# Chunked scan of a state-space layer: TensorE issues a head pair's outputs ahead of the row products of the pair two further on

## The chip, the cores and the metric

The kernel is one program on one core of a Trainium2 chip. The metric is device microseconds for one execution of the whole program. Three timed runs of the kernel before gave 2722.53, 2725.86 and 2726.41 us; their median, 2725.86 us, is the time that the change is measured against.

## The reference, cut to what matters

The program computes two transformer-like layers, for 512 tokens of width 1024: a stick-breaking attention layer with memory cross-attention and a convolutional feed-forward part, then a Mamba-2 layer and a sparse attention layer, each with a gated feed-forward part. Everything is fp32. The change touches the Mamba-2 scan only:

```
def ssd_scan(x, bm, cm, dt_raw, dt_bias, a_log):     # 32 heads of 64, 4 groups of 8 heads, state 128
    ...
        acs = jnp.cumsum(dtk * A, axis=1)
        seg = acs[:, :, None, :] - acs[:, None, :, :]
        decay = jnp.exp(jnp.where(causal, seg, -jnp.inf))            # one matrix per head
        xdt = xk * dtk[..., None]
        cb = jnp.einsum("blgn,bsgn->blsg", ck, bk)                   # one matrix per group
        y_intra = jnp.einsum("blsg,blsgj,bsgjp->blgjp", cb, decay, xdt)
    ...
    y = (y + d_skip[:, None] * xs)
    y = y * jax.nn.silu(z)
    y = rmsnorm(y in groups of 512 channels, norm_g)
    return y @ w_out
```

The kernel takes all 512 tokens as one chunk, so there is no state from an earlier chunk.

## The kernel before

Each engine has its own written-out instruction stream and they meet through semaphores; nothing is scheduled automatically. TensorE (PE) takes its instructions strictly in the order of the code, and so do ScalarE (ACT), VectorE (DVE) and GpSimd (POOL). An instruction that waits for a semaphore therefore holds up all that stands behind it on its engine.

The scan works through 16 pairs of heads. For a pair p the work goes from engine to engine:

- TensorE, `head_rows(hd)` (L1403, L1409), once for each of the two heads: the cumulative sums of the head are broadcast to all rows by seven matmuls, into one of two slots of three PSUM banks each. A slot must be free: ScalarE must have finished with the user two places back (`decay_exp`, or `cb_out` where that was a group matrix).
- ScalarE, `head_decay(hd)` (L1963): four exponentials from the slot into `decay`, a ring of four heads. From head 4 on it first waits for `pair_y`, that is until TensorE has finished the outputs of the pair two back, whose place in the ring it takes.
- VectorE, `mix(hd)` (L2605): `decay` times the group matrix `cbm`, in place (`mixed`).
- GpSimd: `skip` (L2926) and `xdt` (L2930) for the pair, in rings of two pairs, also behind `pair_y` of the pair two back.
- TensorE, `pair_output(pair)` (L1428, L1431): 32 small products into the one PSUM bank 6. It waits for `mixed`, `xdt_ready`, `skip_ready`, and for `y_gated` of the pair before, since that pair's result must have left bank 6.
- VectorE, `gate` (L2610): bank 6 times the gate, into `zt` (`y_gated`). ScalarE squares it (L1972), and TensorE adds the squares up in `sum_squares` (L1440), two pairs late.

Every fourth pair begins a group. `group_products` (L1393) makes the group matrix in a slot, and ScalarE copies it out (L1952); the next slot user but one waits for that copy. When four pairs are summed, ScalarE makes the group's inverse root (two activation table loads, L1979 and L1981), VectorE scales the four results with it (`full`, L2615), ScalarE writes a high part (L1986) and VectorE a low part (L2176, `low`). The output projection `ssm_out` (L694 to L696) follows the scan on TensorE and takes these parts.

TensorE's own order around the change is the loop in `scan` (L1451): in the turn of a pair it issues the row products of the pair two further on, then the outputs of the pair, then `sum_squares` for the pair two back.

Of the kernel before, what the change touches and what calls it, by code (L numbers as in the profile page):

```python
# [182 lines left out]
def build(nc, a, out):  # L183
# [505 lines left out]
    def _(pe):  # L689
# [8 lines left out]
        def banks_out(free=bank_free):  # L698

            pe.wait_ge(free, turns.seen.get(free.name, 0) + FREE0)  # L700
# [686 lines left out]
        def group_products(g):  # L1387

            n = ROW_USERS.index(("cb", g))
            row_slot_free(n)  # L1390
            for kb in (0, 1, 3, 2):
                bank, c0, _, w = decay_strip(n % 2, kb)
                last = nc.tensor.matmul(ps[:, bank, c0:c0 + w], bct[:, g, P * kb:P * kb + P],  # L1393
                                        bct[:, 4 + g, P * kb:SEQ], start=kb != 3, stop=True, skip_group_check=True)
            last.then_inc(cb_ready, 1)

        def head_rows(hd):

            n = ROW_USERS.index(("head", hd))
            row_slot_free(n)  # L1400
            for kb in (0, 1, 3, 2):
                bank, c0, _, w = decay_strip(n % 2, kb)
                nc.tensor.matmul(ps[:, bank, c0:c0 + w], pick[:, hd:hd + 1].to_broadcast([P, P]), acs_t[:, P * kb:SEQ],  # L1403
                                 start=kb != 3, stop=False, skip_group_check=True)
            for kb, twice in ((0, 1), (1, 2), (2, 1)):

                bank, c0, _, w = decay_strip(n % 2, kb)
                blocks = ps[:, bank, :].rearrange("p (b c) -> p b c", c=P)[:, 0:1 + 3 * (twice - 1):3, :]
                last = nc.tensor.matmul(blocks, causal_b[:], ident_b[:].unsqueeze(1).to_broadcast([P, twice, P]),  # L1409
                                        start=False, stop=True, skip_group_check=True)  # L1410
            last.then_inc(acs_rows, 1)

        def pair_output(pair):

            g, bank = pair // 4, 6
            pe.wait_ge(skip_ready, pair + 1)
            pe.wait_ge(xdt_ready, pair + 1)
            pe.wait_ge(mixed, 2 * pair + 2)
            if pair:
                pe.wait_ge(y_gated, pair)  # L1420
            for kb in range(TB):
                for part in range(2):
                    for side in range(2):
                        hd, half = 2 * pair + side, slice(HD * side, HD * side + HD)
                        x = tok[:, g, kb, HD * (hd % HPG):HD * (hd % HPG) + HD]
                        off, n = D_OFF[kb], SEQ - P * kb
                        if part == 0:
                            nc.tensor.matmul(ps[half, bank, P * kb:SEQ], xdt[:, pair % 2, kb, half], decay[:, hd % 4, off:off + n],  # L1428
                                             start=kb == 0, stop=False, skip_group_check=True)
                        else:  # L1430
                            last = nc.tensor.matmul(ps[half, bank, P * kb:P * kb + P], x, skip[:, pair % 2, side, :],  # L1431
                                                    start=False, stop=kb == TB - 1, skip_group_check=True)
            last.then_inc(pair_y, 1)

        def sum_squares(c):

            pe.wait_ge(y_squared, c + 1)
            if c % 4 == 0 and c:
                pe.wait_ge(squares_out, c // 4)
            nc.tensor.matmul(ps[:, 7, :], share[:], sq[:, c % 2, :], start=c % 4 == 0, stop=c % 4 == 3,  # L1440
                             skip_group_check=True).then_inc(squares_in, 1)

        def scan():

            pe.wait_ge(acs_lo, 1)
            pe.wait_ge(bc_copied, 8)
            banks_out()
            group_products(0)
            for hd in range(4):
                head_rows(hd)  # L1450
            for pair in range(HEAD_PAIRS):  # L1451
                ahead = pair + 2
                if ahead < HEAD_PAIRS:
                    if ("cb", ahead // 4 + 1) in SLOT_OF and ahead % 4 == 3:
                        group_products(ahead // 4 + 1)
                    head_rows(2 * ahead)
                    head_rows(2 * ahead + 1)
                pair_output(pair)
                if pair >= 2:
                    sum_squares(pair - 2)  # L1460
            sum_squares(HEAD_PAIRS - 2)
# [55 lines left out]
        feature_pairs(1, acth, actl, free=conv_done, out=False)  # L1517
        gates_and_sums()
        scan()
        ssm_out()  # L1520
        gated_ffn(scaled, mods=2)
# [1510 lines left out]
```

## Time and profile before

| quantity | value |
|---|---|
| median of three timed runs | 2725.86 us |
| the profiled execution's own time | 2727.47 us |
| its span in the profile | 2725.8 us |
| TensorE (matmuls) busy | 2560.2 us, 94% |
| VectorE busy | 1349.3 us, 50% |
| ScalarE busy | 1068.2 us, 39% |
| GpSimd busy | 206.5 us, 8% |
| scan, from its first group product to the first product of `ssm_out` | 1207.61 to 1349.75 us |

All times of the trace are microseconds from the span's start. A busy share of the whole program says little on one stage, so the scan is read by itself: its windows, its waits and its instructions in order of time. A pair's turn is measured from one `gate` (L2610) to the next, since that is what the end of the pair's outputs releases.

### The profile page before, as it was taken

Reading aid. Unit: us, or ns where it says so; the run is one execution under the profiler, and the core shown is the slowest. Engines: PE = TensorE matmul, PEld = TensorE weight load, DVE = VectorE, ACT = ScalarE, POOL = GpSimd, SP = SyncE. Lnnn points to the kernel's source line nnn. Section 1 sums busy time; section 2 is a strip of 40 time slices with the busy share of each in tenths; the row PEclk is TensorE's granted clock in tenths of the full one; section 3 lists DMA queues with packets and bytes.
Section 4 is the critical chain, followed back from the end, with each engine's and each line's share of the span. In section 5 each row is a group of like instructions: output and inputs, shape, how many; then the busy total and the mean of one; then the engine's idle time right before and its main releaser. Section 6 shows DMA issues by size and latency. Waiting matters only on the chain.

```text
span 2725.8 us, 35075 instructions
## 1 busy us (share of the span) xinstructions
PE 2560.2 (94%) x13316; PEld 2079.8 (76%) x13316; DVE 1349.3 (50%) x1870; ACT 1068.2 (39%) x1569; POOL 206.5 (8%) x249
## 2 busy tenths in 40 slices
PE   6979899999999989998899999999988889999999
PEld 5856588788887778774588888888875767888887
DVE  5764447678853365424535633244535454533323
ACT  2235532335552255435535333233424554533322
POOL 1101101010000000001101000010001111100000
PEclk8989999999999999999999999999979999999999
DMA  6740053435423222220024422322311000232232
GB/s 239 265 154 1 16 197 132 145 112 187 154 85 103 90 80 93 87 83 1 1 101 139 154 93 87 108 91 94 100 51 24 16 23 15 71 106 94 85 108 78
DMA packets 178691, 263.21 MB, mean 97 GB/s; under 512 B 8232, under 2 KB 127904, under 8 KB 178592
## 3 DMA queue, kind: packets, MB, share of 16 engines
q1 hardware_dynamic: 156608, 194.00, 21.6%
q0 software_dynamic: 15232, 58.72, 6.1%
q10 hardware_dynamic: 6752, 9.09, 1.0%
q8 instruction: 71, 1.16, 0.2%
q14 instruction: 28, 0.23, 0.0%
HBM read 255.51 MB, written 2.10 MB: 95 GB/s over the span
## 4 chain that ended last, share of the span: by engine, by line
PE 80%; DVE 8%; ACT 6%; issue 3%; POOL 2%; DMA 0%; ACTq 0%; DVEq 0%; SPq 0%; POOLq 0%
PE ps L694 22%; PE ps L696 21%; PE ps L695 21%; PE ps L1321 3%; PE ps L917 2%; ACT decay L1963 2%; DVE wlo L2172 1%; PE ps L971 1%; PE ps L1428 1%; PE ps L1237 1%; DVE actl L2176 1%; PE ps L1263 1%; DVE modulated L2255 1%; PE ps L889 1%; ACT whi L1552 1%
## 5 line engine op out<-in xcount | busy, mean ns | idle before, releaser
L2172 DVE TENSOR_TENSOR wlo<-raw,whi 128x2048 fp32r<-128x2048 f32 x180 | 412.2, 2291 | 713.9 <-ACT whi L1552 713.9
L694 PE MATMUL ps<-acth,wlo 128*128 128x512 f32 (+1 forms) x1888 | 702.7, 372 | 26.1 <-DVE actl L2176 12.5
L696 PE MATMUL ps<-acth,whi 128*128 128x512 f32 (+1 forms) x1888 | 695.8, 369 | 0.0
L695 PE MATMUL ps<-actl,whi 128*128 128x512 f32 (+1 forms) x1888 | 695.7, 368 | 0.0
L1552 ACT ACTIVATE whi<-raw 128x2048 fp32r<-128x2048 f32 x180 | 343.6, 1910 | 568.8 <-PE ps L696 568.8
L694 PEld LDWEIGHTS ps<-acth,wlo 128*128 128x128 f32 x1888 | 357.3, 189 | 89.6 <-DVE actl L2176 15.0
L696 PEld LDWEIGHTS ps<-acth,whi 128*128 128x128 f32 x1888 | 357.3, 189 | 59.7
L695 PEld LDWEIGHTS ps<-actl,whi 128*128 128x128 f32 x1888 | 357.5, 189 | 59.3 <-issue 1.2
L694 PE MATMUL ps<-whi,hid_l 128*128 128x512 f32 x528 | 207.7, 393 | 5.2 <-DVE conv_t L2431 3.4
L695 PE MATMUL ps<-wlo,hid_h 128*128 128x512 f32 x528 | 206.0, 390 | 0.0
L696 PE MATMUL ps<-whi,hid_h 128*128 128x512 f32 x528 | 206.0, 390 | 0.0
L2189 DVE SCALAR_TENSOR_TENSOR macc<-mraw,c_silu,macc 128x256 f32<-128x256 f32 x336 | 137.7, 478 | 0.0
L694 PE MATMUL ps<-whi,actl 128*128 128x512 f32 (+1 forms) x320 | 120.4, 376 | 3.3 <-DVE actl L2176 1.6
L694 PEld LDWEIGHTS ps<-whi,hid_l 128*128 128x128 f32 x528 | 99.6, 189 | 27.4 <-DVE conv_t L2431 3.9
L696 PE MATMUL ps<-whi,acth 128*128 128x512 f32 (+1 forms) x320 | 117.9, 369 | 0.0
L695 PE MATMUL ps<-wlo,acth 128*128 128x512 f32 (+1 forms) x320 | 117.8, 368 | 0.0
L695 PEld LDWEIGHTS ps<-wlo,hid_h 128*128 128x128 f32 x528 | 99.6, 189 | 20.9 <-issue 0.5
L696 PEld LDWEIGHTS ps<-whi,hid_h 128*128 128x128 f32 x528 | 99.4, 188 | 20.7
L1321 PE MATMUL ps<-diag,pn 128*128 128x128 f32 x640 | 92.4, 285 | 20.0 <-POOL diag L2997 14.8
L1321 PEld LDWEIGHTS ps<-diag,pn 128*128 128x128 f32 x640 | 80.0, 193 | 35.9 <-issue 28.3
L2176 DVE TENSOR_TENSOR pnt_l<-ps,pnt_h 128x512 fp32r<-128x512 f32 (+1 forms) x96 | 55.2, 600 | 89.0 <-ACT pnt_h L2074 89.0
L2431 DVE SCALAR_TENSOR_TENSOR conv_t<-ps,cols,conv_t 128x511 f32<-128x511 f32 (+1 forms) x88 | 63.5, 746 | 58.6 <-ACT conv_t L1792 55.1
(330 smaller groups left out, 3647.5 us busy)
## 6 DMA issues: line engine op xcount, KB each, us to landing
mraw<-in_mod_w POOLq DMA_DIRECT2D x48, 1024.0 KB, 5.5
raw<-in_ffn_w_in SPq DMA_DIRECT2D x44, 1024.0 KB, 4.9
raw<-in_ffn_up SPq DMA_DIRECT2D x22, 1024.0 KB, 4.9
raw<-in_ssm_w_in SPq DMA_DIRECT2D x20, 1024.0 KB, 5.0
raw<-in_ffn_w_out SPq DMA_DIRECT2D x20, 1024.0 KB, 4.8
raw<-in_sb_win SPq DMA_DIRECT2D x12, 1024.0 KB, 5.0
raw<-in_ffn_down SPq DMA_DIRECT2D x10, 1024.0 KB, 4.8
raw<-in_xa_wkv SPq DMA_DIRECT2D x8, 1024.0 KB, 5.0
```

Of the source, the lines that this page charges most:

```text
L694: nc.tensor.matmul(o, ll, rh, start=start, stop=False, skip_group_check=True)
L695: nc.tensor.matmul(o, lh, rl, start=False, stop=False, skip_group_check=True)
L696: return nc.tensor.matmul(o, lh, rh, start=False, stop=stop, skip_group_check=True)
L889: last = nc.tensor.matmul(ps[:, 6, 2 * u + j:2 * u + j + 1], macc[:, u, P * j:P * j + P], ones_c[:], start=True, stop=True, skip_group_che ...
L917: return nc.tensor.matmul(ps[:, bank, c0:c0 + keys_of(sb)], k_t[half, pair, P * sb:P * sb + P], q_t[half, pair, P * sb:SEQ], start=start, ...
L1321: last = nc.tensor.matmul(ps[:, 4 + (3 * n + r) % 2, P * b:P * b + P], pn[:, n % 2, off:off + P], diag[:, n % 2, tb, :], start=b == 0, sto ...
L1552: nc.scalar.activation(whi[:, slot, :], raw[:, slot, :], ACT.Copy).then_inc(hi_ready, 1)
L1963: last = nc.scalar.activation(decay[:, hd % 4, off:off + w], ps[:, bank, c0:c0 + w], ACT.Exp, bias=neg_acs[:, kb, hd:hd + 1])
L2172: nc.vector.tensor_tensor(wlo[:, slot, :], raw[:, slot, :], whi[:, slot, :].bitcast(F32), ALU.subtract) \
L2176: return nc.vector.tensor_tensor(dst, src, hi.bitcast(F32), ALU.subtract)
L2189: last = nc.vector.scalar_tensor_tensor(out=o, in0=w, scalar=c, in1=o, op0=ALU.mult, op1=ALU.add)
L2431: last = nc.vector.scalar_tensor_tensor(out=x, in0=ps[:, 2 * u + j, 0:SEQ - shift], scalar=w, in1=x, op0=ALU.mult, op1=ALU.add)
```

## The change

The call of `pair_output(pair)` goes from behind the row products (and the group product, in the turns that have one) to ahead of them. Nothing else is edited, no wait is added or taken away, and the instructions of ScalarE, VectorE, GpSimd and SyncE keep their order.

```diff
             for hd in range(4):
                 head_rows(hd)
             for pair in range(HEAD_PAIRS):
+                pair_output(pair)
                 ahead = pair + 2
                 if ahead < HEAD_PAIRS:
                     if ("cb", ahead // 4 + 1) in SLOT_OF and ahead % 4 == 3:
                         group_products(ahead // 4 + 1)
                     head_rows(2 * ahead)
                     head_rows(2 * ahead + 1)
-                pair_output(pair)
                 if pair >= 2:
                     sum_squares(pair - 2)
             sum_squares(HEAD_PAIRS - 2)
```

On TensorE, in the middle of the scan, the kernel before has this order from the end of one pair's outputs to the start of the next pair's (L1403 and L1409 are one head's row products, L1440 is the sum of squares, L1428 and L1431 are a pair's outputs):

```order
L1431 MATMUL ps<-skip,tok 64x128 x2
L1440 MATMUL ps<-sq,share 128x512 [waits y_squared]
L1403 MATMUL ps<-acs_t,pick 128x512 [waits decay_exp]
...
L1409 MATMUL ps<-ident_b,causal_b 128x128
L1403 MATMUL ps<-acs_t,pick 128x512 [waits decay_exp]
...
L1428 MATMUL ps<-decay,xdt 64x512 [waits mixed,y_gated,xdt_ready,skip_ready]
```

The changed kernel has this one at the same place of TensorE's stream:

```order
L1431 MATMUL ps<-skip,tok 64x128 x2
L1403 MATMUL ps<-acs_t,pick 128x512 [waits decay_exp]
...
L1409 MATMUL ps<-ident_b,causal_b 128x128
L1403 MATMUL ps<-acs_t,pick 128x512 [waits decay_exp]
...
L1440 MATMUL ps<-sq,share 128x512 [waits y_squared]
L1428 MATMUL ps<-decay,xdt 64x512 [waits mixed,y_gated,xdt_ready,skip_ready]
```

The sum of squares has gone from ahead of the row products to behind them, and what looks the same is not: the row products between the outputs of pairs p and p+1 are those of pair p+3 before, and those of pair p+2 now.

At the start of the loop on TensorE, behind the row products of heads 0 to 3, the outputs of pair 0 now stand ahead of the row products of head 4:

```order
 L1409 MATMUL ps<-ident_b,causal_b 128x128
+L1428 MATMUL ps<-decay,xdt 64x512 x2
+L1431 MATMUL ps<-skip,tok 64x128 x2
+L1428 MATMUL ps<-decay,xdt 64x384 x2
+L1431 MATMUL ps<-skip,tok 64x128 x2
+L1428 MATMUL ps<-decay,xdt 64x256 x2
+L1431 MATMUL ps<-skip,tok 64x128 x2
+L1428 MATMUL ps<-decay,xdt 64x128 x2
+L1431 MATMUL ps<-skip,tok 64x128 x2
 L1403 MATMUL ps<-acs_t,pick 128x512
```

All eight rows of a pair's outputs have moved up by the row products of two heads.

## Rows read from the trace of the kernel before

**Rows 1.** Window: length, busy PE, PEld, DVE, ACT, POOL, granted clock, DMA.
```profile
1226.40:1345.10 118.70, 95.85 (x686) 57.02 (x688) 68.28 (x60) 76.01 (x157) 24.25 (x28) 0.99 0.00 1
```

**Rows 2.** Waits from 1226.4 to 1350: waiter, releaser, total, times, longest.
```profile
ACT decay L1963 <- PE ps L1431: 47.8, 12, 6.3
PEld ps L1403 <- ACT decay L1963: 25.3, 20, 2.2
```

**Rows 3.** Timeline of one ordinary turn: start, duration, engine, line, count.
```profile
1241.21 1.08 PE L1428 MATMUL ps<-decay,xdt 128*64 128x512 f32 x4
...
1244.39 1.13 PE L1440 MATMUL ps<-sq,share 128*128 128x512 f32 x2
1244.51 0.69 DVE L2610 TENSOR_TENSOR zt<-ps,zt 128x512 f32<-128x512 f32 x1 [2.89 <-PE ps L1431]
...
1244.57 3.46 ACT L1963 ACTIVATE decay<-ps,neg_acs 128x512 f32<-128x512 f32 x8 [3.96 <-PE ps L1431]
...
1246.41 0.91 PE L1403 MATMUL ps<-acs_t,pick 128*128 128x512 f32 x4 [0.89 <-ACT decay L1963]
1246.46 3.10 DVE L2605 TENSOR_TENSOR decay<-decay,cbm 128x1280 f32<-128x1280 f32 x2 [1.26 <-ACT decay L1963]
...
1248.08 0.91 PE L1403 MATMUL ps<-acs_t,pick 128*128 128x512 f32 x4 [0.53 <-ACT decay L1963]
...
1249.15 1.08 PE L1428 MATMUL ps<-decay,xdt 128*64 128x512 f32 x4
```

**Rows 4.** Timeline of one turn with a group product.
```profile
1260.38 0.69 DVE L2610 TENSOR_TENSOR zt<-ps,zt 128x512 f32<-128x512 f32 x1 [2.89 <-PE ps L1431]
...
1262.28 2.43 PE L1393 MATMUL ps<-bct 128*128 128x512 f32 x8 [0.89 <-ACT decay L1963]
...
1266.15 0.91 PE L1403 MATMUL ps<-acs_t,pick 128*128 128x512 f32 x4 [0.58 <-ACT cbm L1952]
...
1270.52 0.69 DVE L2610 TENSOR_TENSOR zt<-ps,zt 128x512 f32<-128x512 f32 x1 [5.09 <-PE ps L1431]
```

**Rows 5.** Timeline of the start, to the first pair's gate.
```profile
1214.68 3.10 DVE L2605 TENSOR_TENSOR decay<-decay,cbm 128x1280 f32<-128x1280 f32 x2 [3.10 <-ACT decay L1963]
...
1218.49 1.54 PE L1403 MATMUL ps<-acs_t,pick 128*128 128x512 f32 x4
...
1220.25 1.52 PE L1403 MATMUL ps<-acs_t,pick 128*128 128x512 f32 x4
...
1226.44 0.69 DVE L2610 TENSOR_TENSOR zt<-ps,zt 128x512 f32<-128x512 f32 x1 [4.74 <-PE ps L1431]
```

**Rows 6.** Window at the start, columns as in group 1.
```profile
1224.00:1224.50 0.50, 0.50 (x8) 0.41 (x6) 0.00 (x0) 0.00 (x0) 0.00 (x0) 0.82 0.00 0
```

**Rows 7.** Timeline of the end of the scan and the first product behind it.
```profile
1336.26 0.69 DVE L2610 TENSOR_TENSOR zt<-ps,zt 128x512 f32<-128x512 f32 x1 [2.31 <-PE ps L1431]
...
1342.43 1.10 PE L1440 MATMUL ps<-sq,share 128*128 128x512 f32 x2 [1.99 <-ACT group_rstd L1979]
1343.46 0.20 PEld L1428 LDWEIGHTS ps<-decay,xdt 128*64 128x64 f32 x4 [0.76 <-issue]
...
1348.45 0.69 DVE L2610 TENSOR_TENSOR zt<-ps,zt 128x512 f32<-128x512 f32 x1 [3.43 <-PE ps L1431]
...
1349.75 0.79 PE L694 MATMUL ps<-whi,yl 128*128 128x512 f32 x1
```

**Rows 8.** Timeline: VectorE and ScalarE work that the later turns add.
```profile
1274.58 1.28 ACT L1979 ACT_TABLE_LOAD   x1
...
1278.51 3.46 ACT L1963 ACTIVATE decay<-ps,neg_acs 128x512 f32<-128x512 f32 x8
...
1286.99 2.26 DVE L2615 SCALAR_TENSOR_TENSOR zt<-zt,cols,group_rstd 128x512 f32<-128x512 f32 x2
```

**Rows 9.** Timeline behind the last pair, where VectorE has no GpSimd work beside it.
```profile
1349.06 2.06 DVE L2615 SCALAR_TENSOR_TENSOR zt<-zt,cols,group_rstd 128x512 f32<-128x512 f32 x3
...
1351.04 2.49 DVE L2176 TENSOR_TENSOR yl<-zt,yh 128x512 fp32r<-128x512 f32 x4
```

## The prediction, written before the changed kernel was run

> **What bounds the kernel now.** I read the waits of the scan first, then one ordinary turn and one group turn in order of time, then both ends, and the windows last, for the clock. The page's 94% of TensorE says nothing here: in the scan TensorE's matmuls are busy 95.85 of 118.70 us and ScalarE 76.01 [rows 1], so no engine is full. The waits name a ring: ScalarE's exponentials wait 47.8 us in 12 waits for the end of a pair's outputs, and the weight loads of the row products wait 25.3 us for the exponentials [rows 2].
>
> One turn shows how the ring closes [rows 3]. The outputs of a pair start at 1241.21 and release ScalarE at 1244.57, 3.36 us later. TensorE's next row products want a slot that these exponentials must first read: the first head's start at 1246.41, the second's at 1248.08, so 3.51 us after ScalarE began. The outputs of the next pair stand behind them in TensorE's order and start 1.07 us later, at 1249.15. The turn is 3.36 + 3.51 + 1.07 = 7.94 us. The reader is to see that these outputs needed nothing from those exponentials: their own two heads had been mixed a turn earlier. They are late only because of what stands in front of them. A turn with a group product takes 10.14 us, 1260.38 to 1270.52 [rows 4].
>
> **What the change does to an ordinary turn.** Nothing is added or removed; the terms are gaps. Behind the outputs of pair p now come the row products of pair p+2, not p+3. Their slots were read by the exponentials of pair p+1, a turn ago, so TensorE doesn't wait. The turn becomes TensorE's own work:
> - outputs, start to the next instruction's start, 1241.21 to 1244.39: 3.18 us [rows 3];
> - row products of two heads. The 1.07 us from a head's start to the outputs' start [rows 3] is the upper end for one. The lower end is 0.88: at half clock one head follows another after 1.76 us [rows 5]. I take 1.0 each, nearer to the row at full clock: 2.0 us;
> - sum of squares: 1.03 us, 1342.43 to 1343.46 [rows 7]. (Where it stands behind outputs it looks shorter, as its start overlaps their end.)
>
> Sum 6.2 us, against 7.94.
>
> The price of the move is on ScalarE: its exponentials for pair p+2 now wait for the outputs of p and also for the row products behind them, some 1.2 us. Does that come back? The chain from the end of outputs p is: row products 1.2, exponentials 3.5 (the second head's last, rows 3), mix of the second head 1.5 (half of 3.10), so pair p+2 is ready 6.2 to 6.3 us after outputs p end. It is needed at two turns less one set of outputs, 12.4 - 3.2 = 9.2 us. Slack 2.9 us. The other condition is bank 6: the gate stands on VectorE behind both mixes of the pair p+1, which end about at the end of outputs p (6.3 - 6.2), and takes 0.69; the next outputs start 3.0 us after that end. Slack some 2.2 us. Sums of squares wait for squares that are a turn old. GpSimd's work for a pair has a whole turn.
>
> **The group turns.** Outputs end, the group product starts at once; from its start to the second head's row products is 1262.28 to 1266.15 = 3.87 us, ScalarE's copy being on that path [rows 4]. Then 1.07 (head to next), 1.03 (squares) and 3.18 (outputs): 9.15 us against 10.14. In the first group turn there are no squares yet: 8.1. The gain is small here because the copy out of the slot stays in the path.
>
> **The sum.** From the first gate to that of pair 13 the trace has 13 turns, 1226.44 to 1336.26 = 109.8 us, which is 3 x 10.14 and 10 x 7.94 [rows 5, 7]. After: the first turn without squares 5.2, the group turns 8.1 + 9.15 + 9.15, nine ordinary turns 9 x 6.2 = 55.8. Together 87.4 us, 22.4 less.
>
> The end: before, pairs 14 and 15 take 1336.26 to 1348.45, 12.2 us, with a wait of 1.99 us for the group root [rows 7]. After: 6.2, and for pair 15 outputs 3.2, squares 1.0 and what is left of that wait. ScalarE comes to the root's first half 1.2 (row products) + 3.3 + 0.5 + 2.0 (table load and logarithm, half of the 3.93 from 1274.58 to 1278.51, rows 8) = 7.0 us after outputs 13, TensorE after 6.2: a wait of 0.8. Sum 11.2, a gain of 1.0.
>
> The start: outputs of pair 0 can go at 1218.4, where the row products of head 4 started at 1218.49; the mixes they need ended at 1217.8 [rows 5]. The granted clock is at half, the 1.2 GHz level, and comes back to 2.4 GHz at about 1224.2 (0.82 in that half microsecond, rows 6); TensorE is as busy until then as before, so I leave that moment where it is. So of 3.3 us of work at full clock 2.9 are done by 1224.2 and the gate comes at about 1224.6, not 1226.44: 1.8 us.
>
> 22.4 + 1.0 + 1.8 = 25.2 us. Each turn has hand-overs between kinds of instructions that no row shows in the new order; at 0.1 us in each of twelve they take back 1.2. I forecast 24 us. What follows the scan is TensorE's from 1349.75 on [rows 7], and its first two weight blocks lie in SBUF long before, so it shifts as a whole. The profiled execution's own time is 2727.47 us around a span of 2725.8; it would become 2703.5. On the median, 1.6 us lower, that is 2725.9 - 24 = 2701.9 us.
>
> **What could be dearer.** VectorE in turns from 7 on has mixes 2.9, gate 0.6, one `full` 0.7 and one `low` 0.6 (a third and a quarter of rows 9), 4.8 us. But two `full` beside GpSimd's work take 2.26 us [rows 8], and three without it 2.06 [rows 9]: the one that meets GpSimd costs 1.6, so 0.9 more. That is 5.7 of 6.2 us.
>
> The Trainium skill ("SBUF — State Buffer", section "Who interferes with whom") says that a VectorE instruction with two SBUF inputs contends with a GpSimd one that reads SBUF, and that whoever came first has the shared port for its whole instruction. The 1.6 us agrees. By that rule a shorter turn could make a mix lose such a stretch as well, 4.8 + 2 x 0.9 = 6.6 us, over TensorE's 6.2: 0.4 in each of nine turns, 4 us lost, 2706. It is counted within the second rival.
>
> **The rivals.**
> 1. TensorE fills its turns, -24 us: 2702. Its own range is 2699 to 2706: the row products at 0.88 or 1.07 each move 26 of them by 3 and 2 us, and the last pair's outputs may again take 5.0 us to their gate (1343.46 to 1348.45, rows 7) and not 3.3, which my sum has left out.
> 2. VectorE and ScalarE take over as the bound from turn 7 on. For it: turn 7, 11 and 15 have the root's 3.9 us on ScalarE [rows 8], which uses up most of the gate's 2.2 us of slack, and the mixes come nearer to GpSimd's work in a shorter turn. Against: the sums above, 5.7 us on VectorE. Priced by VectorE's fullest turn, mixes 2.9, gate 0.7, two `full` 2.26, `low` 0.6 and 0.7 of waiting, 7.1 us: nine turns at 0.9 more are 8 us, so -16: 2710.
> 3. The scan ends earlier and nothing behind it does, because the projection waits for something timed from elsewhere: 2726. Against it: DMA share is 0.00 through the scan [rows 1], so nothing is on the way that could be late.
> 4. Slower: the granted clock. In the scan it is 0.99 of full although TensorE pauses about 2 us in each turn, but at the start it is at half [rows 6]. At half clock a turn's 6.2 us are 12.4. It decides once more than 59 us of the scan are at half clock, for each such us costs half of one, and 24 + 5.5 us must be lost for a slower kernel. A whole scan so, some 100 us of work done in 200, would end at 2800. Against: the change takes pauses away.
>
> **How the numbers follow.** Chances: 0.75, 0.18, 0.05, 0.02. A difference under 0.2%, 5.5 us, can't be told from none here. The first two cases are faster by far more, and of the third's spread a little is too: faster 0.94, same 0.04, slower 0.02. The range takes the first case's and goes to the second's price and a little over: 2698 to 2711.
>
> **What would show it.** In the profile after, ScalarE's exponentials wait for L1409, not L1431; the 25.3 us of waits of L1403 for exponentials are gone but for the copies (L1952) in three turns; gates come 6.2 us apart, 9.2 in group turns; the scan's PE share goes from 0.81 to over 0.95. Rival 2 shows as TensorE waiting for L2605 or L2610 ahead of L1428 from turn 8 on. Gates under 6.0 or over 6.5 us apart in the early turns would mean that I mis-sized TensorE's own turn, and a wait for `mixed` in turns 2 to 6 that the chain of 6.3 us is wrong.

## The result and the profile after

Four runs of the changed kernel gave 2695.52 to 2700.37 us, median 2698.56, beside 2724.2 us for the kernel before in the same comparison: 25.6 us less, ratio 0.9903, 95% interval 0.9889 to 0.9917. A second build of it on another occasion gave 2697.47 against 2725.46 us, ratio 0.9902 (0.9886 to 0.9919). The forecast was 24 us less, 2701.9 us, in a range from 2698 to 2711. The first median is inside it, 0.6 us above its lower end; that of the second build is 0.5 us below it. Of the 3.3 us between 2701.9 and 2698.56, 1.7 are the kernel before, whose median was 2725.86 us when the forecast was made and 2724.2 us in the comparison; 1.6 are the change.

| | before | after |
|---|---|---|
| profiled execution, own time | 2727.47 | 2698.84 |
| span | 2725.8 | 2697.1 |
| first group product of the scan | 1207.61 | 1206.06 |
| first product of the projection | 1349.75 | 1320.18 |
| scan, between them | 142.1 | 114.1 |
| from there to the end of the span | 1376.1 | 1376.9 |

The spans differ by 28.7 us: 28.0 in the scan, 1.6 ahead of it and -0.9 behind it, which the change doesn't touch. Outside the scan, where no kernel of this document differs, the spans of all thirteen traces lie between 2577.0 us (squares first) and 2586.8 us (between heads). So the traces tell what happens in the scan more finely than the timed runs of the whole program do.

In the window of the scan (columns as in [rows 1]) TensorE is now busy for 108.23 of 113.73 us, 0.95, against 0.82 in the whole scan of the kernel before (0.81 without its start, [rows 1]). ScalarE went from 0.62 to 0.77, VectorE from 0.55 to 0.67:

```profile
1206.06:1319.79 113.73, 108.23 (x797) 69.14 (x798) 75.81 (x67) 87.41 (x178) 28.37 (x28) 0.97 0.03 11
```

The waits after, from 1200 to 1330 (columns as in [rows 2]):

```profile
ACT decay L1963 <- PE ps L1409: 14.2, 10, 3.7
...
DVE zt L2610 <- PE ps L1431: 3.8, 4, 1.7
...
PEld ps L1403 <- ACT cbm L1952: 3.3, 4, 0.9
PEld ps L1403 <- ACT decay L1963: 2.5, 3, 2.2
...
PE ps L1440 <- ACT group_rstd L1979: 1.1, 1, 1.1
```

ScalarE no longer waits for outputs, 47.8 us before, but for the row products behind them, 14.2 us. TensorE's loads for row products waited 28.0 us for the exponentials, 25.3 of them behind the first gate [rows 2]; 2.5 are left, 2.2 of them in one wait at the start. What still stops TensorE are the group copies and one wait for the group root.

One ordinary turn in the timeline after answers to [rows 3]:

```profile
1243.44 1.08 PE L1428 MATMUL ps<-decay,xdt 128*64 128x512 f32 x4
...
1246.62 0.89 PE L1403 MATMUL ps<-acs_t,pick 128*128 128x512 f32 x4
1246.74 0.69 DVE L2610 TENSOR_TENSOR zt<-ps,zt 128x512 f32<-128x512 f32 x1
...
1247.56 0.88 PE L1403 MATMUL ps<-acs_t,pick 128*128 128x512 f32 x4
1247.79 3.46 ACT L1963 ACTIVATE decay<-ps,neg_acs 128x512 f32<-128x512 f32 x8 [2.10 <-PE ps L1409]
1248.51 1.08 PE L1440 MATMUL ps<-sq,share 128*128 128x512 f32 x2
1249.52 1.08 PE L1428 MATMUL ps<-decay,xdt 128*64 128x512 f32 x4
```

TensorE has no wait in it. Outputs take 3.18 us to the next start, the first head's rows 0.94, the second's 0.95, the squares 1.01: 6.08 us, against 7.94. ScalarE starts its exponentials 4.35 us after the outputs' start, 3.36 before: that is the price of the move, and nobody is late for it.

In the later turns VectorE is nearly full, and a gate (the multiplication that takes a pair's outputs out of bank 6) no longer marks the end of the outputs, since it comes late. The timeline there:

```profile
1266.10 3.10 DVE L2605 TENSOR_TENSOR decay<-decay,cbm 128x1280 f32<-128x1280 f32 x2 [0.99 <-ACT decay L1963]
...
1267.97 1.70 POOL L2926 TENSOR_TENSOR skip<-ident,heads 128x256 f32<-128x256 f32 x1 [4.45 <-PE ps L1431]
...
1269.11 0.69 DVE L2610 TENSOR_TENSOR zt<-ps,zt 128x512 f32<-128x512 f32 x1
...
1270.72 1.08 PE L1428 MATMUL ps<-decay,xdt 128*64 128x512 f32 x4
```

The outputs ended at about 1267.9, the gate began at 1269.11, 1.2 us late behind two mixes, and ended at 1269.80, 0.9 us before the outputs of the next pair. So VectorE was close to being the bound and did not become it. I therefore read turns from one pair's outputs to the next, by their starts on TensorE. From the timelines, one kernel to a row (the edits follow below), in us; "first" is from the first group product to the outputs of pair 0, "last" from the last pair's outputs to the projection:

```
                      first  0-1   1-2   2-3   3-4   4-5   5-6   6-7   7-8   8-9   9-10  10-11 11-12 12-13 13-14 14-15 last   scan
before                14.54 11.13  7.93  7.94  7.94 10.14  7.93  7.93  7.93 10.21  7.93  7.94  7.93  7.93  4.23  6.27  6.29  142.1
after                 10.67  6.42  8.12  6.08  6.09  6.08  9.04  6.07  6.09  6.08  9.04  6.07  6.09  6.09  6.08  5.41  4.60  114.1
squares last          14.54 11.18  7.92 10.48 10.39 10.13 10.36 10.96 10.59 11.22  8.84 11.93 10.67 10.63  4.23  6.50  6.01  166.6
squares last, busy    14.55 11.14  7.93 10.47  8.85 10.28  8.84 11.94  9.24 10.28  8.84 11.00  8.85  8.84  5.53  4.97  5.90  157.5
squares first         10.69  6.43  8.12  6.03  6.04  6.04  8.98  7.69  6.04  6.02  8.98  7.71  6.03  6.02  6.03  7.17  5.39  119.4
between heads         12.81 10.34  6.26  6.26  6.25  8.40  6.25  7.81  6.25  8.41  6.26  7.79  6.25  6.25  5.16  5.34  4.60  120.7
first pair only       10.68 12.40  8.50  8.99  7.94 10.14  7.93  7.93  7.92 10.22  7.92  7.94  7.94  7.93  4.23  6.27  4.60  139.5
all but first         14.00  4.13  8.13  6.09  6.08  6.08  9.04  6.08  6.09  6.07  9.04  6.08  6.08  6.09  6.09  5.40  4.60  115.2
before, more rows     14.88 10.14  9.22  7.94  7.93 10.14  7.94  7.92  7.93 10.22  7.93  7.93  7.93  7.93  4.23  6.54  5.97  142.7
after, more rows      10.31  5.63  8.12  6.56  6.55  6.54  9.04  6.55  6.55  6.54  9.04  6.55  6.55  6.54  6.55  5.41  4.59  117.6
squares fill          10.67  6.46  8.12  6.08  6.09  6.08  8.18  6.10  6.36  6.08  8.19  6.09  6.37  6.08  6.09  4.13  5.65  112.8
fill and start        11.53  5.99  8.13  6.08  6.09  6.08  8.19  6.09  6.35  6.08  8.19  6.09  6.35  6.08  6.08  4.13  5.65  113.2
```

The gain of 28.0 us from the first two lines: 3.9 at the start and 23.4 in the 13 turns to pair 13 (110.8 to 87.4); 1.0 is lost in the two turns to pair 15 (10.5 to 11.5), because the outputs of pair 14 followed those of pair 13 at once before and have the last row products ahead of them now; and 1.7 is gained in the last stretch.

### The profile page after: what moved, and what is told of

Same layout as the page of the kernel before. It is cut to its first block, busy times and chain, and to the rows that moved or that the text cites. A ratio compares the mean times of both kernels' runs of the same rounds, so it can differ in the third digit from the quotient of the medians.

```text
span 2697.1 us, 35075 instructions
## 1 busy us (share of the span) xinstructions
PE 2552.4 (95%) x13316; PEld 2079.4 (77%) x13316; DVE 1347.8 (50%) x1870; ACT 1067.6 (40%) x1569; POOL 210.5 (8%) x249
## 4 chain that ended last, share of the span: by engine, by line
PE 81%; DVE 8%; ACT 4%; issue 3%; POOL 2%; DMA 0%; ACTq 0%; DVEq 0%; SPq 0%; POOLq 0%
PE ps L694 22%; PE ps L696 22%; PE ps L695 22%; PE ps L1321 3%; PE ps L917 2%; PE ps L1428 1%; DVE wlo L2172 1%; PE ps L971 1%; PE ps L1237 1%; PE ps L1403 1%; DVE actl L2176 1%; PE ps L1263 1%; DVE modulated L2255 1%; PE ps L889 1%; ACT whi L1552 1%
```

## The experiments

My theory: the kernel before is held by a ring that closes only through TensorE's order, the outputs standing behind row products that wait for the exponentials which the last outputs released. Moved ahead, they leave TensorE bound by its own work. Rivals: the sums of squares, which moved too; the start alone; VectorE or ScalarE as the new bound.

**Squares last.** The order before, with only the sums of squares moved.

```diff
+                if grouped:
+                    if pair >= 3:
+                        sum_squares(pair - 3)
+                    group_products(ahead // 4 + 1)
                 if ahead < HEAD_PAIRS:
-                    if ("cb", ahead // 4 + 1) in SLOT_OF and ahead % 4 == 3:
-                        group_products(ahead // 4 + 1)
                     head_rows(2 * ahead)
                     head_rows(2 * ahead + 1)
+                if pair >= 3 and not grouped:
+                    sum_squares(pair - 3)
                 pair_output(pair)
-                if pair >= 2:
-                    sum_squares(pair - 2)
+            sum_squares(HEAD_PAIRS - 3)
             sum_squares(HEAD_PAIRS - 2)
```

> The kernel before, with only the other thing that the change did to TensorE's order: each sum of squares goes behind the row products (in the three turns with a group product it goes ahead of them), while the outputs stay last in the turn. Theory (the ring through TensorE's order): a sum of squares that stood beside the wait for the exponentials now stands in the ring, so an ordinary turn grows from 7.94 by 0.92 us to 8.9 us, in some nine turns, and in two of them TensorE also waits for the group root, 1 us more: the kernel is 8 to 11 us slower than before, ratio 1.003 to 1.004. Rival (moving the sums of squares was part of the gain): faster than before by some us, turns under 7.9 us.

Measured: 2747.68 us against 2725.01, ratio 1.0083 (1.0064 to 1.0103), 22.7 us slower: the sign of the theory and twice its size. The squares' move earns nothing by itself. (What it is worth behind outputs that come first is the experiment after the next.) But ordinary turns are 10.4 to 10.7 us, not 8.9, except one of 8.84 us. The timeline of TensorE in one of them, and the windows over it (the eighth number, behind POOL's, is the granted clock):

```profile
1245.05 0.89 PE L1403 MATMUL ps<-acs_t,pick 128*128 128x512 f32 x4 [1.94 <-ACT decay L1967]
...
1246.72 1.50 PE L1403 MATMUL ps<-acs_t,pick 128*128 128x512 f32 x4 [0.54 <-ACT decay L1967]
...
1248.46 1.95 PE L1440 MATMUL ps<-sq,share 128*128 128x512 f32 x2
```

```profile
1245.00:1246.00 1.00, 0.95 (x7) 0.82 (x7) 0.90 (x1) 1.00 (x3) 0.00 (x0) 1.00 0.00 0
1246.00:1247.00 1.00, 0.46 (x4) 0.28 (x2) 0.89 (x2) 0.67 (x3) 0.00 (x0) 0.90 0.02 8
1247.00:1248.00 1.00, 1.00 (x4) 0.83 (x3) 1.00 (x1) 0.00 (x0) 0.00 (x0) 0.50 0.00 0
...
1250.00:1251.00 1.00, 1.00 (x5) 0.34 (x6) 0.00 (x0) 0.49 (x1) 0.00 (x0) 0.89 0.00 0
```

The clock falls to its 1.2 GHz level for some 3.4 us of the turn, while the second head's rows and the squares run, both in the ring. With the squares behind the rows TensorE pauses 1.94 us ahead of the first head's rows. In the kernel before the squares stood in that pause and left 0.89 us of it [rows 3], and the clock stayed; only its first turns have the long pause, for want of squares.

The turn of 8.84 us has the same pause, and there the clock stayed at full speed:

```profile
1313.00:1323.00 10.00, 7.52 (x57) 4.81 (x59) 5.55 (x5) 3.45 (x9) 2.15 (x2) 1.00 0.01 2
```

```profile
1319.18 0.90 PE L1403 MATMUL ps<-acs_t,pick 128*128 128x512 f32 x4 [1.94 <-ACT decay L1967]
...
1321.82 1.08 PE L1440 MATMUL ps<-sq,share 128*128 128x512 f32 x2
```

So the ring is as long as its terms say when the clock holds, and the clock does not fall behind each such pause.

**Squares last, busy.** The test of that: the same kernel, with products in the pause. They add to columns of the bank in which the sums of squares stand, so this kernel's output isn't the reference's.

```diff
+        def keep_busy():
+            for _ in range(3):
+                nc.tensor.matmul(ps[:, 7, 0:256], ident[:], causal6[:, 0:256], start=False, stop=True,
+                                 skip_group_check=True)
...
                 pair_output(pair)
+                if pair % 4 != 2:
+                    keep_busy()
```

> The kernel with the squares last (the outputs as before, sums of squares behind the row products) took turns of 10.4 us where the ring gave 8.9, and its granted clock was 0.83 in most windows. Here TensorE gets more work: three products of 256 columns, 1.3 us, directly behind each pair's outputs, into the sums' bank (so the sums of squares and the output aren't the reference's), in all turns but those in which ScalarE reads that bank. They fall in the 2 us in which TensorE waits for the exponentials. Theory (the miss was the clock, which falls because TensorE pauses in that wait and the work that follows is in the ring): the clock stays at 1.00, ordinary turns are 8.8 to 9.0 us, the kernel is 8 to 13 us slower than before, ratio 1.003 to 1.005, in spite of more work than the one without. Rival (the ring has another part that I missed): turns of 10.4 us and more, ratio 1.008 or above.

Measured: 2743.73 us against 2725.16, ratio 1.0061 (1.0044 to 1.0079), above the expected ratios. Its scan is 9.1 us shorter than without the extra work; of the whole program the timed runs show 4 us, with intervals that overlap, so the gain from more work is shown in the scan only. By turns the theory holds: behind pairs that got the work, the turns that have neither a group product nor a root are 8.84 or 8.85 us, one 9.24. Behind pairs 2, 6 and 10, which didn't, they are 10.47, 11.94 and 11.00 (the last two with the root's wait). I had forgotten those three turns in the expectation. In one turn with the work:

```profile
1254.64 1.56 PE L1438 MATMUL ps<-causal,ident 128*128 128x256 f32 x6
1256.66 0.91 PE L1403 MATMUL ps<-acs_t,pick 128*128 128x512 f32 x4 [0.45 <-ACT decay L1975]
...
1258.33 0.90 PE L1403 MATMUL ps<-acs_t,pick 128*128 128x512 f32 x4 [0.53 <-ACT decay L1975]
...
1259.30 1.08 PE L1446 MATMUL ps<-sq,share 128*128 128x512 f32 x2
1260.31 1.08 PE L1428 MATMUL ps<-decay,xdt 128*64 128x512 f32 x4
```

and the granted clock in the two windows around it, first over a turn without the work and then with it:

```profile
1243.00:1253.00 10.00, 7.51 (x48) 4.45 (x46) 3.67 (x3) 4.09 (x9) 1.62 (x2) 0.83 0.00 1
1253.00:1263.00 10.00, 9.02 (x72) 5.78 (x70) 3.68 (x3) 4.09 (x9) 1.62 (x2) 1.00 0.01 2
```

The second head's rows take 0.90 and the squares 1.08, not 1.50 and 1.95. So the ring is 7.94 + 0.91 = 8.85 us, as its terms say, and what was over was the clock. In this trace the clock fell in none of the turns that got the work (in the one of 9.24 us it was still down from the turn before).

**Squares first.** The changed kernel, with `sum_squares(pair - 2)` directly behind `pair_output(pair)`:

```diff
                 pair_output(pair)
+                if pair >= 2:
+                    sum_squares(pair - 2)
...
-                if pair >= 2:
-                    sum_squares(pair - 2)
```

> The changed kernel with each sum of squares moved back directly behind the outputs, ahead of the row products. Theory: TensorE is full in both orders, so ordinary turns stay at 6.1 us; but the sums for pairs 4 and 8 wait for ScalarE's group root, now with the row products behind them and not only outputs, 1 to 1.5 us in each of two turns. 22 us faster than before, ratio 0.992, 2 to 4 us behind the changed kernel. Rival (the place of the squares matters in each turn): a turn over 6.5 us, less than 18 us faster.

Measured: 2700.98 us against 2725.01, ratio 0.9916 (0.9894 to 0.9939); 24.0 us. Ordinary turns 6.03 us, and 7.69 and 7.71 in the two turns with the root, as the wait of 1.63 us shows:

```profile
1261.32 1.10 PE L1440 MATMUL ps<-sq,share 128*128 128x512 f32 x2 [1.63 <-ACT group_rstd L1979]
```

The scan is 5.3 us longer than in the changed kernel, a little more than I wrote, 3.2 in those two turns and most of the rest at the end (7.17 + 5.39 against 5.41 + 4.60). Where the squares stand is worth nothing in an ordinary turn, once the outputs are first. But these 5.3 us of the scan are what their place behind the row products earns in the changed kernel, by shorter waits for the group root and full clock at the end; the change's gain is not the outputs' move alone.

**Between heads.** The order before, with the outputs moved past one head's rows only:

```diff
                     head_rows(2 * ahead)
+                pair_output(pair)
+                if ahead < HEAD_PAIRS:
                     head_rows(2 * ahead + 1)
-                pair_output(pair)
```

> The kernel before, with the outputs moved up past one head's row products only: first head, outputs, second head, squares. Theory: the ring still closes through TensorE's order but over one head's exponentials: 3.36 + 1.84 + 1.07 = 6.3 us in an ordinary turn, 8.3 in a group turn (the copy of the group matrix no longer stands ahead of the outputs), about 7.7 in the two turns behind a group root. 20 to 23 us faster than before, ratio 0.992. Rival (the outputs must be ahead of all row products for TensorE to get past the wait): half the gain or less, turns of 7 us and more. Rival (TensorE's own work is the bound in both): the same turns as the changed kernel, 6.1 and 9.0 us.

Measured: 2704.97 us against 2725.01, ratio 0.9921 (0.9904 to 0.9937); 20.0 us. Turns 6.25, with a group product 8.40, with a root 7.80; 6.3, 8.3 and 7.7 were expected. One turn in the timeline of TensorE:

```profile
1242.09 1.08 PE L1428 MATMUL ps<-decay,xdt 128*64 128x512 f32 x4
...
1245.27 0.90 PE L1403 MATMUL ps<-acs_t,pick 128*128 128x512 f32 x4
...
1246.24 1.08 PE L1440 MATMUL ps<-sq,share 128*128 128x512 f32 x2
1247.28 0.90 PE L1403 MATMUL ps<-acs_t,pick 128*128 128x512 f32 x4
...
1248.34 1.08 PE L1428 MATMUL ps<-decay,xdt 128*64 128x512 f32 x4
```

The first head's rows start 5.19 us after the outputs did, which is 3.36 us to the exponentials and 1.83 for those of one head; their weight load waits 0.79 us for ScalarE. The outputs follow 1.06 us later. This experiment tells the ring's formula from "TensorE is full in any order", if by little: the turn is 0.17 us longer than TensorE's own 6.08 in the changed kernel and 0.22 us longer than the 6.03 of squares first. It is shorter in group turns, where the copy is out of the path.

**First pair only.** The order before, and for pair 0 the changed one.

```diff
+                if pair == 0:
+                    pair_output(pair)
...
-                pair_output(pair)
+                if pair > 0:
+                    pair_output(pair)
```

> The kernel before, with only the outputs of pair 0 moved ahead of the row products of head 4; all later turns as before. Theory: what the first gate gains (1.8 to 3.6 us) the second turn gives back, since the exponentials of pair 2 then wait for row products that stand behind the outputs: the second gate comes some 11 us after the first, not 10.1, and the kernel is 1 to 2 us faster than before, which the timing can't tell. Rival (the start is a gain of its own): 3 to 4 us faster, and the second gate 10.1 us behind the first.

Measured: 2725.52 us against 2725.01, ratio 1.000 (0.999 to 1.0009). In the trace pair 0 is 3.9 us early and the next three turns are 1.3, 0.6 and 1.1 us longer (in the last two the clock fell behind the long pause of the turns without squares); to the outputs of the last pair the whole is 1.0 us ahead of before. The start is not a gain of its own. (The scan of this trace is 2.6 us shorter than before, 1.7 of them in the last stretch, where the clock held; the timed runs show nothing of it.)

**All but first.** The complement: pair 0 as before, all others as changed (the two conditions above exchanged).

> The changed kernel with the outputs of pair 0 left behind the row products of heads 4 and 5, where they were before; all later turns as changed. Theory: nearly the whole gain is in the turns: 23 to 26 us faster than before, ratio 0.991, with ordinary turns of 6.1 us and the first gate as late as before. Rival (the start and the early return of the clock carry a seventh of the gain): 4 us and more behind the changed kernel.

Measured: 2699.64 us against 2725.84, ratio 0.9911 (0.9891 to 0.993); 26.2 us. The scan is 1.1 us longer than the changed kernel's: pair 0 comes 3.3 us later and the next turn is 2.3 us shorter, since pair 1 was ready long before.

**More rows, in both orders.** The widest row product of each pair's first head three times, same values, in the kernel before and in the changed one.

```diff
             for kb in (0, 1, 3, 2):
                 bank, c0, _, w = decay_strip(n % 2, kb)
-                nc.tensor.matmul(ps[:, bank, c0:c0 + w], pick[:, hd:hd + 1].to_broadcast([P, P]), acs_t[:, P * kb:SEQ],
-                                 start=kb != 3, stop=False, skip_group_check=True)
+                for _ in range(3 if kb == 0 and hd % 2 == 0 else 1):
+                    nc.tensor.matmul(ps[:, bank, c0:c0 + w], pick[:, hd:hd + 1].to_broadcast([P, P]),
+                                     acs_t[:, P * kb:SEQ], start=kb != 3, stop=False, skip_group_check=True)
```

> The kernel before with more work for TensorE: the first, 512 columns wide row product of each pair's first head is issued three times and not once (the repeats overwrite the same values). Theory: they fall in TensorE's wait for the second head's exponentials, 0.53 us in each turn, so 0.45 us of work costs nothing: turns stay at 7.94 us, the kernel within 2 us of before. Rival (TensorE's work already counts in the kernel before): turns of 8.4 us, 6 us slower.

> The changed kernel with the same repeats: the first row product of each pair's first head three times. Theory (TensorE is now full): each turn grows by the whole 0.45 us, from 6.1 to 6.55 us, 6 us in 14 turns; 18 to 21 us faster than before, ratio 0.993. Rival (VectorE or ScalarE bound the later turns): turns from 7 on stay at their length, 3 us or less in all.

Measured: before with them 2724.73 us against 2725.84, ratio 0.9997 (0.9987 to 1.0007), ordinary turns 7.92 to 7.94 (9.22 once, in an early one, where the clock fell). The repeats have filled the second wait, and the second head's rows start 1.68 us behind the first's, 1.67 before [rows 3]:

```profile
1251.65 1.36 PE L1404 MATMUL ps<-acs_t,pick 128*128 128x512 f32 x6 [0.89 <-ACT decay L1964]
...
1253.33 0.90 PE L1404 MATMUL ps<-acs_t,pick 128*128 128x512 f32 x4
```

After with them 2701.0 us, ratio 0.9916 (0.9896 to 0.9935), 24.8 us under before and not 18 to 21. The slope per turn is as expected, 0.46 us, from 6.09 to 6.55. In the timeline of TensorE, where L1404 are the rows, in the changed kernel:

```profile
1246.07 1.36 PE L1404 MATMUL ps<-acs_t,pick 128*128 128x512 f32 x6
...
1247.48 0.88 PE L1404 MATMUL ps<-acs_t,pick 128*128 128x512 f32 x4
```

It counts only in ten turns, 4.6 us. In group turns the repeats lie beside the wait for the copy (9.04 in both), and the start was 1.2 us shorter, the clock having held there. The scan is 3.5 us longer. So 0.45 us of TensorE's work is free in the order before and costs its whole length in the changed one, also in the turns from 7 on, where VectorE or ScalarE would have hidden it if they were the bound.

**Squares fill.** An attempt to fill TensorE's remaining waits; and the changed kernel again beside it.

```diff
+                squares = [pair - 2] if 2 <= pair < HEAD_PAIRS - 2 else []
...
                     head_rows(2 * ahead)
+                    if grouped:
+                        for c in squares:
+                            sum_squares(c)
+                        squares = []
                     head_rows(2 * ahead + 1)
-                if pair >= 2:
-                    sum_squares(pair - 2)
-            sum_squares(HEAD_PAIRS - 2)
+                for c in squares:
+                    sum_squares(c)
+            for c in range(HEAD_PAIRS - 4, HEAD_PAIRS - 1):
+                sum_squares(c)
```

> The changed kernel once more, on the same chip and with the same runs of before as the next one. Theory: ratio 0.9895 to 0.991 against before; ordinary turns 6.1 us, group turns 9.0. If the early return of the clock at the start (at 1219.3 us, 13.2 us behind the first group product) was by chance, it comes at another place here and the first gate moves by 1 to 2 us.

> The changed kernel with its two waits on TensorE filled: in group turns the sum of squares goes between the two heads' row products, where TensorE waits 0.57 us and more for the copy of the group matrix, and the sum of squares of pair 12, which waits 1.14 us for the group root, goes behind the last outputs. Theory: the group turns of pairs 6 and 10 go from 9.0 to 8.2 us and the last turn from 5.4 to 4.3: 2 to 3 us faster than the changed kernel in the trace, 0.1%, at the edge of what the timing tells. Rival (ScalarE, whose exponentials follow the copy, is as late): group turns give their 0.8 us back in the next turns, less than 1 us in all.

Measured: changed kernel again ratio 0.9902 (above), turns within 0.07 us of its first trace's. With the fill 2697.53 us, ratio 0.9897 (0.988 to 0.9913). Group turns 8.18 us instead of 9.04, where 0.27 of the 0.86 came back two turns later; the last turn 4.13 instead of 5.41, where 1.05 of the 1.28 came back at once. The row in the group turn, the squares between the heads' rows:

```profile
1255.76 0.99 PE L1403 MATMUL ps<-acs_t,pick 128*128 128x512 f32 x4
1256.15 1.36 ACT L1959 ACTIVATE cbm<-ps 128x512 f32<-128x512 f32 x3 [3.40 <-PE ps L1393]
1256.59 0.40 PE L1409 MATMUL ps<-ident_b,causal_b 128*128 128x128 bf16 x3
1256.82 1.08 PE L1440 MATMUL ps<-sq,share 128*128 128x512 f32 x2
...
1257.56 0.96 PE L1403 MATMUL ps<-acs_t,pick 128*128 128x512 f32 x4
```

The scan is 1.3 us shorter, not 2 to 3, and the timing can't tell it from the changed kernel.

**Fill and start.** The same, with the first row product of heads 0 and 2 three times.

> The changed kernel with squares in the waits of the group turns and behind the last outputs, and besides with the first row product of heads 0 and 2 issued three times (same values), at the start, where TensorE waits for ScalarE. With such repeats in all pairs the clock did not fall at the start and the second pair's outputs started 1.1 us earlier. Theory: scan 111.5 to 112.0 us, against 112.8 with the squares alone and 114.1 in the changed kernel; in the timing 0.1% under the changed kernel's 0.9902 of before, at the edge of what it tells. Rival (that the clock held was chance): it falls to half at about 1213 us as before, and the scan takes 112.8 us or more.

Measured: 2697.22 us against 2725.16, ratio 0.989 (0.9873 to 0.9907). The rival is right: the clock fell at the start all the same, 0.56 in the window from 1213 to 1218, and the scan took 113.2 us. With more rows in all pairs TensorE had the same instructions up to that moment, and there the clock held in the changed kernel and fell in the kernel before. So the repeats do not decide it. The ratio is the lowest of all, but its interval overlaps with those of the two kernels above.

## Why the prediction was right in its mechanism and wrong in terms of its sum

**The ring.** Its reading was right in each point that was tested: the turn before is the sum of three terms, the order of TensorE alone closes it, and other orders gave the turn that the same terms give, 6.25 between heads, 8.85 with squares in it.

**The steps that failed.** In the prediction's own terms, from gate to gate, the traces show 28.0 us where the sum had 24.0:

| term | forecast, us | measured, us |
|---|---|---|
| turns from the gate of pair 0 to that of pair 13 | 22.4 | 23.7 |
| hand-overs, taken off | -1.2 | 0, no row shows any |
| end, to the gate of pair 15 | 1.0 | 0.7 |
| start, to the gate of pair 0 | 1.8 | 3.6 |

The start was mis-sized most, by 1.8 us: the step "I leave that moment where it is", for the return of the clock, did not hold. The hand-overs are next, 1.2 us that no row had asked for, and then TensorE's own turn, 0.12 us too long. The timed gain, 25.6 us, is nearer to the 24 than the trace's 28.0.

**The ordinary turn.** Forecast 6.2 us, measured 6.08. The outputs' 3.18 was exact, the two heads' rows 1.89 and not 2.0, the squares 1.01 and not 1.03. The 0.1 us of hand-over per turn that was taken off besides did not exist: in each turn one kind of work follows the other without a gap. The 13 turns were 87.4 us in the forecast, ahead of the hand-overs, and 86.1 from gate to gate (1221.28 to 1307.38); nine ordinary turns explain 1.1 of the difference. The first turn was as forecast, 5.2 us from the end of one pair's outputs to the end of the next's (TensorE's next instructions start at 1221.15 and 1226.32); the 6.4 us in the table of turns goes by starts, and has the first outputs at half clock in it. By the sign that the prediction gave, gates under 6.0 us apart in the early turns, it had mis-sized the turn; but gates were 5.72 us apart there (1234.93 to 1240.65) because the earlier one came late, and the sign was a bad one.

**Group turns.** 8.1 and 9.15 forecast, 8.12 and 9.04 measured.

**The price on ScalarE.** The chain of 6.3 us was right (6.2 in the turn shown above, to the end of the second mix) and no turn waits for `mixed`. The gate's slack was 2.2 us by the sum and 0.9 in the fullest turn, where the root had held ScalarE.

**The end.** Forecast 11.2 us from the gate of pair 13 to that of 15, measured 11.5 (1307.38 to 1318.88). The wait for the root was 1.14 us and not 0.8. The last outputs ran at full clock, as the sum had assumed:

```profile
1313.47 0.69 DVE L2610 TENSOR_TENSOR zt<-ps,zt 128x512 f32<-128x512 f32 x1
...
1314.56 1.10 PE L1440 MATMUL ps<-sq,share 128*128 128x512 f32 x2 [1.14 <-ACT group_rstd L1979]
1315.58 1.08 PE L1428 MATMUL ps<-decay,xdt 128*64 128x512 f32 x4
...
1318.76 1.98 PE L1440 MATMUL ps<-sq,share 128*128 128x512 f32 x4
```

**The start.** The sum left the return of the clock where it was, 16.6 us behind the first group product; it came at 13.2, seen in the windows (0.71 in the half microsecond from 1219.0):

```profile
1218.50:1219.00 0.50, 0.50 (x8) 0.50 (x6) 0.34 (x1) 0.13 (x1) 0.00 (x0) 0.50 0.00 0
1219.00:1219.50 0.50, 0.50 (x6) 0.23 (x4) 0.50 (x1) 0.00 (x0) 0.00 (x0) 0.71 0.00 0
```

The gate of pair 0 was 15.2 us behind the first group product and not 18.8: 3.6 us, forecast 1.8. Is that the change's doing? The runs leave it open. The return came at one of two times in the traces in which the clock had fallen. In all six in which the outputs of pair 0 stand ahead of the rows of head 4 it came at 13.2 or 13.3 us. In the six with another order there it came at 13.3 in two (all but first, and before with more rows) and at 16.6 in four (before, squares last, its busy version, between heads). All but first has the same instructions as the kernel before up to that point, so the early return comes without the change too; whether the change favours it isn't shown. And the first pair's 1.8 or 3.6 us are not a gain by themselves, as the first-pair kernel showed: without them, in all but first, the scan was 1.1 us longer.

**What the clock added.** Before, the last outputs ran at half clock: 6.29 us from their start to the projection, 4.60 after. This goes with the wait for the group root ahead of them. In the five kernels in which it is 2.0 us (before, squares last, squares first, before with more rows, first pair only) the last outputs were slow in four; in the five in which it is 1.1 us (the changed one twice, all but first, between heads, after with more rows) in none. In the other three the wait is 0.7 us or there is none, and the last outputs ran at full clock; their last stretch is longer by the work that was put there. So these 1.7 us are probably the change's, through a shorter wait, and the sum had them: it set the changed kernel's last outputs at full clock. At the start 1.5 us of the trace's 28.0 may be chance: 0.5 ahead of pair 0 (14.0 in all but first) and 1.0 in the turn behind it (10.14 in before with more rows, whose clock was back at 13.3). That leaves 26.5 to 28.0 us for the change, where the terms of the forecast added up to 25.2 ahead of the hand-overs and the ratio of the timed runs gives 26 (23 to 30).

**Rivals.** VectorE or ScalarE as the bound: not so, by the slope of more rows. But near: VectorE is busy 9.84 of 10 us in the window 1273 to 1283. The port: the rule of the Trainium skill ("SBUF — State Buffer", section "Who interferes with whom") that who comes first holds it through showed the other way round than I had priced it. GpSimd's `skip` came to a running mix and took 1.70 us where it takes 0.61 alone, as in the lines at 1267.97 above, while the mix kept its time; GpSimd had a turn to spare. A `full` behind GpSimd's work took 1.50 us, about the 1.6 of before. The scan ending early for nothing: not so, the work behind it takes 1376.9 us and took 1376.1, and moved up as a whole. The clock as a danger: it didn't fall in the changed kernel's turns, but the rival was real; it cost the squares-last kernel more than half of its loss. The prediction had held against it that TensorE pauses about 2 us in each turn without harm. That is a sum of pauses, of which the longest in an ordinary turn was 0.89 us [rows 3]; behind single ones of 1.94 us the clock fell in most turns.

## What to carry to other kernels

Where an engine takes its instructions in order, look in the trace for one whose inputs have long been ready and that starts right behind one that was waiting: the turn is then the sum along a ring which the order has made, and issuing the ready one first is worth the whole wait, down to the engine's own work. Add up that work beforehand, and that of the next engine, since the gain ends there. And know which work fills the pause of such a ring: moving it out lengthened this ring by its length and cost TensorE its clock in most turns besides.

## What was not expected of the hardware

TensorE's clock fell again in turn after turn of a loop. With a pause of 1.94 us in each turn the granted clock was 0.83 over the turn and turns took 10.4 us; with 1.3 us more work in that pause it was 1.00 and the turns took 8.85 us. In one turn it stayed at 1.00 in spite of the pause, and that turn took 8.84 us. A stretch of a kernel can be faster for more work. At the start, with the same order of instructions there, the clock came back either 13.3 (all but first) or 16.6 us (before) behind the first group product, so a difference of 1 to 2 us between two single traces of this kernel need not be the order's.
